# Grouped-query projection of seven token tiles in three rounded products

## The chip, the cores and the metric

The kernel runs on one core of one Trainium2 chip. The metric is the device time of one execution in microseconds (us); the median of three timed executions is what counts. The core has four computing engines that run their own instruction streams side by side and meet at semaphores: TensorE (PE in the rows; PEld is its loading of the stationary operand), VectorE (DVE), ScalarE (ACT) and GpSimd (POOL). SyncE (SP) issues the DMA transfers. Each engine works strictly in the order in which its instructions are written: one that waits holds all behind it.

## What is computed

The reference is one step of a two-layer network on 1024 sample tokens and 128 prompt tokens, all in float32. Each layer normalises its input, projects it with one wide matrix and hands slices of the result to four mixers: latent attention, grouped-query attention, differential attention and a long convolution. Cut to the part that matters here:

```python
h = rmsnorm(x, lp['norm_pre']) * (1.0 + scale) + shift
z = h @ lp['w_in']                         # 1024 input features
(..., g_q, g_k, g_v, g_gate, ...) = jnp.split(z, ...)
gq = rmsnorm(g_q.reshape(b, n, 4, 64), lp['gqa_q_norm'])
gk = rmsnorm(g_k.reshape(b, n, 2, 64), lp['gqa_k_norm'])
gv = g_v.reshape(b, n, 2, 64)
gq, gk = axial_rope(gq, row, col), axial_rope(gk, row, col)   # sample tokens only
o_gqa = gqa_blocks(...)                    # softmax(q k / 8) v
```

The 256 columns of `g_q`, 128 of `g_k` and 128 of `g_v` make one block of 512 output columns. Its product with the normalised tokens is the grouped-query projection.

## The kernel before

**Tiling.** The 1152 tokens are nine tiles of 128 (0 to 7 sample, 8 prompt). The normalised input lies in on-chip memory with features on the partitions, `hT`, eight groups of 128 features by 1152 tokens. Weights come through two slots of 1024 by 512 numbers, `W`. One projection of a tile (`project`, called at line 1247) is eight matmuls of 128x128 against 128x512, one for each feature group, summed in one of eight banks of accumulator memory (`psum`). They are float32 matmuls; a float32 matmul stands in the trace as two records, so a projection is 16 records.

**Stages.** A layer is cut into stages by barriers (`stage_end`) at which the engines wait for each other. The grouped-query stage is from the barrier after the latent attention up to the next one after the grouped-query attention. Tiles 0 and 1 are projected in the last steps of the latent attention stage (line 1043). What follows in the stage on each engine:

- TensorE, lines 1240 to 1261: a gate product of 512 columns (`gate`, 16 records); then for i from 1 to 9 `parts_turned(i - 1)`, eight transposes of the split queries and keys of tile i - 1, and, up to i = 7, `project` of tile i + 1. At i = 9 a second gate product of the same size comes ahead of the transposes. More gate products follow, the transposes of the cached keys, and the attention.
- ScalarE, lines 1667 to 1687: for each tile i, copy the projection out of its bank (384 columns for queries and keys, line 1675, and 128 for values, line 1677), then take the transposed parts of tile i - 1 into `q_parts` and `k_parts` with rounding (lines 1653 to 1661).
- VectorE, lines 2272 to 2294: for each tile i the chain that makes split queries and keys: squares, sum over heads (2283), the variance (1727), then a wait while GpSimd takes the inverse root, two scalings, the rotation (`rope`, seven instructions), and `split` (2231 to 2256), which ends with the subtraction that lets TensorE's transposes go. A step of `link` waits for the instruction before it. After tile 0 comes the end of a gate (1908).
- GpSimd: clears a part of `k_parts` (2431), then one inverse root for each tile.

All these short helpers record one line: 1722 is any `tensor_tensor` of VectorE, 659 any matmul, 663 any transpose, 2336 any `tensor_tensor` of GpSimd, 426 the barrier.

**Three rounded products elsewhere.** The output projection at the layer's end (`out_product`, line 1048) does for its token tiles 3 to 8 what the change does for the grouped-query projection. A float32 number is taken as the sum of a rounded part (type float32r, made by a ScalarE copy) and a rest (made by a VectorE subtraction, also float32r), and the product is high x high + high x low + low x high, three float32r matmuls in place of one float32 matmul, each a single record. `w_high` and `w_low` are the parts of the weights, `o_high` and `o_low` those of the tokens; lines 1500 and 1509 round, lines 2093 and 2102 subtract.

Of the kernel before, what the change touches and what calls it, by code (L numbers as in the profile page):

```python
# [31 lines left out]
F32 = mybir.dt.float32  # L32
# [5 lines left out]
P = 128  # L38
# [11 lines left out]
WC = 512  # L50
# [77 lines left out]
ROPE_DIFF = (DQ + 128, SPLIT + 2 * 896)  # L128
CKEY_DIFF = SPLIT + 2 * 896 + NT * 128
# [218 lines left out]
def program(nc, I, outs, known=None):  # L348
    with ExitStack() as ctx:  # L349
# [28 lines left out]
        o_low = pieces_of("o_low", [(SGH + TT * GW + slot * D, P) for slot in range(3)], KD)  # L378

# [272 lines left out]
        def _(pe):  # L652
# [33 lines left out]
            for l in S.layers():  # L686
# [131 lines left out]

                def gate(grp, c, c0, f, i, banks):

                    weights(c)
                    tok, n = PARTS[i]
                    ps = claim(("gate", grp, f, i), banks)
                    for k in range(KD):
                        last = mm(ps[:, 0:n], W[:, SLOT[c, 0], k, c0 + f * P:c0 + (f + 1) * P],
                                  hT[:, k, tok:tok + n], k == 0, k == KD - 1)
                    last.then_inc(*K.done(("gate", grp, f, i)))
# [409 lines left out]
                for grp in ("gqa", "diff0", "diff1"):  # L1237
                    vg = "gqa_gate" if grp == "gqa" else "diff_vg"
                    vg0, f = (0, 0) if grp == "gqa" else (GW, int(grp[4]))
                    gate(grp[:4], vg, vg0, f, 0, K.next())  # L1240
                    for i in range(1, TT + 1):
                        if i == TT:
                            gate(grp[:4], vg, vg0, f, 1, K.next())
                        parts_turned(grp, i - 1)
                        t = i + AHEAD[grp] - 1
                        if t < TT and grp == "gqa":
                            project(grp, "proj", t, grp, 0, 512, K.next())
                        elif t < TT:
                            diff_project(grp, t, K.next())
                        elif t == TT and grp == "diff0":  # L1250
                            prompt_values()
# [36 lines left out]
        def _(act):  # L1288
# [14 lines left out]
            for l in S.layers():  # L1303
# [136 lines left out]
                def attention(grp):  # L1440
# [32 lines left out]
                    for g in range(tail_step(grp)):  # L1473
# [5 lines left out]
                        if late(grp, g):  # L1479
                            take(g - 2, 0)  # L1480

# [164 lines left out]
                for grp in ("gqa", "diff0", "diff1"):  # L1646
# [19 lines left out]
                    order = six if grp == "gqa" else [(int(grp[4]), i) for i in range(3)]  # L1666
                    for i in range(TT + 1):
                        if i < TT:
# [46 lines left out]
        def _(v):  # L1715
# [39 lines left out]
            for l in S.layers():  # L1755
# [501 lines left out]

                for grp, nh, n in (("gqa", 6, 64), ("diff0", 8, 32), ("diff1", 8, 32)):
# [6 lines left out]
                    if grp == "diff0":  # L2265
# [5 lines left out]
                        link(nc.vector.tensor_scalar(gcol[:, :], gcol[:, :], lamv[:, 5:6], 0.5, ALU.mult, ALU.mult))  # L2271
                    for i in range(TT + 1):
                        if i == TT:
# [262 lines left out]
```

## Time and profile before

| | us |
|---|---|
| median of three timed runs (2438.95 to 2441.79) | 2441.25 |
| profiled execution | 2435.95 |
| its span, first to last instruction | 2434.2 |
| grouped-query stage of layer 0, start to the second gate product | 598.5 to 662.8 |
| the same of layer 1 | 1800.0 to 1864.3 |

A profile lists what each engine did and when, in us from the start of the span. "Busy" is the time in which an instruction of that engine ran; matmuls are pipelined, so their records overlap, and the pace of a row of matmuls is read from their starts. In a timeline a row is: start, length, engine, line, operation, what is written and read with its size, the count of merged instructions, and in brackets how long the engine had been idle and what released it.

### The profile page before, as it was taken

The page shows a single profiled execution, that of the slowest core. Times are in us where ns is not written, and L with a number is a line of the kernel's source. Part 1 is how long each engine was busy: PE and PEld are TensorE (multiplying, and loading weights), DVE is VectorE, ACT ScalarE, POOL GpSimd, SP SyncE. Part 2 cuts the span into 40 slices and gives each one's busy share as a digit, 9 for nine tenths or more (in the row PEclk, how much of TensorE's full clock was granted, in tenths as well). Part 3 has the DMA queues.
Part 4 walks back from the last instruction along what each step waited for, and adds up shares of the span by engine and source line. Part 5 has one row for each costly group of instructions (what it writes and reads, how often), then busy time and mean ns, then how long its engine had stood idle before and what let it go on. Part 6 is the DMA issues. An engine that isn't in the chain of part 4 may idle for free. (4 is left out here: it accounts for less than half of the span.)

```text
span 2434.2 us, 36385 instructions
## 1 busy us (share of the span) xinstructions
PE 2272.0 (93%) x14536; PEld 1599.2 (66%) x14536; DVE 1317.5 (54%) x2454; ACT 935.4 (38%) x1924; POOL 253.8 (10%) x400
## 2 busy tenths in 40 slices
PE   6999999899999998989999999998999999889898
PEld 3656865685477776864856577657854777768657
DVE  3642764564656466583446337545645654855732
ACT  2332113553155265483224221135521652744721
POOL 0310001000100011011304000010011000110213
PEclk9999999999999999999989999999999999999999
DMA  8710100100020000113275101001001100001022
GB/s 282 262 46 29 57 18 1 54 2 15 2 76 2 4 4 7 36 36 131 79 233 203 53 11 57 18 1 54 1 15 37 41 1 8 1 7 71 1 87 87
DMA packets 75150, 129.64 MB, mean 53 GB/s; under 512 B 25794, under 2 KB 38978, under 8 KB 73348
## 3 DMA queue, kind: packets, MB, share of 16 engines
q1 hardware_dynamic: 73960, 121.65, 14.6%
q10 hardware_dynamic: 1024, 5.67, 0.7%
q8 instruction: 117, 1.92, 0.3%
q14 instruction: 49, 0.40, 0.1%
HBM read 110.10 MB, written 21.92 MB: 54 GB/s over the span
## 5 line engine op out<-in xcount | busy, mean ns | idle before, releaser
L659 PE MATMUL psum<-arena 128*32 128x128 f32 (+9 forms) x9392 | 1505.3, 391 | 63.0 <-issue 11.9
L659 PEld LDWEIGHTS psum<-arena 128*32 128x32 f32 (+3 forms) x9392 | 930.5, 151 | 564.5 <-issue 423.7
L663 PE MATMUL psum<-ident,arena 128*128 128x128 f32 (+1 forms) x2248 | 335.2, 279 | 70.8 <-ACT arena L1543 34.0
L1722 DVE TENSOR_TENSOR arena<-arena 128x256 f32<-128x256 f32 (+10 forms) x710 | 318.8, 493 | 146.6 <-ACT arena L1419 42.6
L663 PEld LDWEIGHTS psum<-ident,arena 128*128 128x128 f32 (+1 forms) x2248 | 254.3, 141 | 155.6 <-issue 101.9
L659 PE MATMUL psum<-k_parts,q_parts 96*128 96x384 f32 (+2 forms) x1000 | 269.8, 366 | 17.1 <-ACT arena L1454 6.0
L2019 DVE TENSOR_REDUCE st<-psum 128x1 f32<-128x1152 f32 (+1 forms) x144 | 177.9, 1237 | 52.3 <-PE psum L659 52.1
L1722 DVE TENSOR_TENSOR arena<-psum,arena 128x512 f32<-128x512 f32 (+2 forms) x116 | 68.1, 596 | 253.3 <-PE psum L659 253.1
L2114 DVE TENSOR_REDUCE st<-psum 128x1 f32<-128x1152 f32 (+1 forms) x144 | 174.0, 1235 | 53.6 <-PE psum L659 53.1
L659 PEld LDWEIGHTS psum<-k_parts,q_parts 96*128 96x128 f32 (+1 forms) x1000 | 171.0, 193 | 34.7 <-issue 16.8
L1454 ACT ACTIVATE arena<-psum,st 128x1152 f32<-128x1152 f32 (+1 forms) x144 | 162.4, 1128 | 51.8 <-DVE st L2019 43.7
L1529 ACT ACTIVATE arena<-psum,st 128x1152 f32<-128x1152 f32 (+1 forms) x144 | 162.5, 1129 | 34.0 <-DVE st L2114 33.6
L1469 ACT COPY arena<-psum 128x512 f32<-128x512 f32 (+1 forms) x244 | 102.1, 433 | 184.9 <-PE psum L663 184.8
L2336 POOL TENSOR_TENSOR st<-st,minus 128x1 f32<-128x1 f32 x72 | 43.7, 607 | 798.2 <-ACT arena L1529 798.2
L2336 POOL TENSOR_TENSOR arena<-arena 128x1024 f32<-128x1024 f32 (+2 forms) x38 | 98.6, 2603 | 189.1 <-DVE arena L1855 138.7
L2033 DVE COPY arena<-psum 128x512 f32<-128x512 f32 (+1 forms) x156 | 93.6, 612 | 28.7 <-PE psum L663 28.7
L1543 ACT COPY arena<-psum 128x512 f32<-128x512 f32 (+1 forms) x200 | 90.3, 470 | 46.4 <-PE psum L663 45.4
L1886 DVE SCALAR_TENSOR_TENSOR arena<-arena,hcw 128x1024 f32<-128x1024 f32 x24 | 30.8, 1285 | 125.9 <-ACT arena L1373 125.5
L2124 DVE SCALAR_TENSOR_TENSOR arena<-arena,st 128x1152 f32<-128x1152 f32 (+1 forms) x72 | 93.0, 1291 | 9.8 <-POOL st L2336 9.8
L1492 ACT ACTIVATE arena<-psum 128x512 f32<-128x512 f32 x36 | 21.5, 598 | 173.3 <-PE psum L659 173.3
L2336 POOL TENSOR_TENSOR st<-st,mhalf 128x1 f32<-128x1 f32 (+2 forms) x72 | 56.2, 780 | 300.8 <-DVE st L1727 300.8
L1653 ACT CAST q_parts<-psum 96x512 fp32r<-96x512 f32 (+1 forms) x54 | 31.7, 588 | 117.0 <-PE psum L663 116.5
(146 smaller groups left out, 1685.8 us busy)
## 6 DMA issues: line engine op xcount, KB each, us to landing
arena<-in_ada_w SPq DMA_DIRECT2D x12, 2048.0 KB, 8.3
arena<-in_w_in SPq DMA_DIRECT2D x10, 2048.0 KB, 9.6
arena<-out_xs SPq DMA_DIRECT2D x36, 512.0 KB, 5.9
out_xs<-arena SPq DMA_DIRECT2D x18, 512.0 KB, 2.6
arena<-in_w_out SPq DMA_DIRECT2D x4, 2048.0 KB, 8.0
out_xs<-in_x ACTq DMA_DIRECT2D x1, 4608.0 KB, 19.2
spectrum_kept<-arena SPq DMA_DIRECT2D x2, 2304.0 KB, 8.6
arena<-spectrum_kept SPq DMA_DIRECT2D x2, 2304.0 KB, 8.4
```

The source lines that it names most:

```text
L659: return nc.tensor.matmul(out, lhsT, rhs, start=start, stop=stop)
L663: return nc.tensor.transpose(out, src, ident[0:n, 0:n])
L1454: nc.scalar.activation(at(buf, nk, w), psum[:, 512 * b0:512 * (b0 + nk)].rearrange("p (c n) -> p c n", c=nk)[:, :, 0:w], ACT.Exp, bias=st[ ...
L1469: nc.scalar.copy(at(SLOTS[grp] + slot(grp, u) * 1152 + 512 * j, nk * P), bank[b][:, 0:nk * P]).then_inc(*S.up("turned_scalar", (grp, number)))
L1529: nc.scalar.activation(at(buf, nk, w), psum[:, 512 * b0:512 * (b0 + nk)].rearrange("p (c n) -> p c n", c=nk)[:, :, 0:w], ACT.Exp, bias=st[ ...
L1543: nc.scalar.copy(at(SLOTS[grp] + slot(grp, u) * 1152 + 512 * j, nk * P), bank[b][:, 0:nk * P]).then_inc(*S.up("turned_scalar", (grp, number)))
L1722: return nc.vector.tensor_tensor(out, a, b, op)
L2019: nc.vector.tensor_reduce(st[:, 16 + x % 4:17 + x % 4], psum[:, 512 * b0:512 * (b0 + nk)].rearrange("p (c n) -> p c n", c=nk)[:, :, 0:w], ...
L2033: nc.vector.tensor_copy(at(SLOTS[grp] + slot(grp, u) * 1152 + 512 * j, nk * P), bank[b][:, 0:nk * P]).then_inc(*S.up("turned_vector", (grp ...
L2114: nc.vector.tensor_reduce(st[:, 16 + x % 4:17 + x % 4], psum[:, 512 * b0:512 * (b0 + nk)].rearrange("p (c n) -> p c n", c=nk)[:, :, 0:w], ...
L2124: nc.vector.scalar_tensor_tensor(p0, p1, c, p0, ALU.mult, ALU.add).then_inc(*S.up("mixed", (grp, u)))
L2336: return nc.gpsimd.tensor_tensor(out, a, b, op)
```

## The change

The projections of the grouped-query block for tiles 2 to 8 (seven of nine) are made as three rounded products. Tiles 0 and 1 stay as they were.

- ScalarE rounds the weight block in two parts of 128x2048 in the last steps of the latent attention, and each token tile (128x1024) in the grouped-query stage: tile 2 ahead of the loop, tile i + 3 at the head of step i, behind a wait for the product of tile i + 1, whose buffer it takes.
- VectorE subtracts: at the stage's start the rest of tile 2 (two instructions of 128x512) and of the weights (two of 128x2048), which overwrite the weights in `W`, and at the head of step i, for i from 1 to 6, the rest of tile i + 2 (two of 128x512).
- TensorE makes 24 float32r matmuls for a tile. The product of tile 2 now stands right behind the first gate product, ahead of the transposes of tile 0, and the product of tile i + 2 (before: i + 1) behind the transposes of tile i - 1.

```diff
@@ tensor engine @@
+                def gqa_project(t, banks):
+                    for part in range(2):
+                        pe.wait_ge(*S.at("gqa_w_low", part))
+                    pe.wait_ge(*S.at("gqa_h_low", t))
+                    ps = claim(("proj", "gqa", t), banks)
+                    for k in range(KD):
+                        wh, wl = (w[k // 4][:, k % 4, :] for w in (gqa_w_high, gqa_w_low))
+                        hh, hl = gqa_h_high[t % 2][:, k, :], gqa_h_low[t % 2][k // 4][:, k % 4, :]
+                        mm(ps[:, :], hh, wh, k == 0, False)
+                        mm(ps[:, :], hh, wl, False, False)
+                        last = mm(ps[:, :], hl, wh, False, k == KD - 1)
+                    last.then_inc(*K.done(("proj", "gqa", t)))
...
                     gate(grp[:4], vg, vg0, f, 0, K.next())
+                    if grp == "gqa":
+                        gqa_project(GQA_SPLIT, K.next())
                     for i in range(1, TT + 1):
...
                         parts_turned(grp, i - 1)
-                        t = i + AHEAD[grp] - 1
+                        t = i + GQA_SPLIT if grp == "gqa" else i + AHEAD[grp] - 1
                         if t < TT and grp == "gqa":
-                            project(grp, "proj", t, grp, 0, 512, K.next())
+                            gqa_project(t, K.next())
@@ scalar engine @@
+                        if grp == "mla" and len(units) + 1 <= g < len(units) + 3:
+                            gqa_round_weights(g - len(units) - 1)
+                def gqa_round_tokens(t):
+                    if t >= GQA_SPLIT + 2:
+                        act.wait_ge(*K.full(("proj", "gqa", t - 2)))
+                    nc.scalar.copy(gqa_h_high[t % 2][:, :, :], hT[:, :, t * P:(t + 1) * P]).then_inc(*S.up("gqa_h_high", t))
...
+                    if grp == "gqa":
+                        gqa_round_tokens(GQA_SPLIT)
                     for i in range(TT + 1):
+                        if grp == "gqa" and i + GQA_SPLIT + 1 < TT:
+                            gqa_round_tokens(i + GQA_SPLIT + 1)
@@ vector engine @@
+                def gqa_weights_rest(part):
+                    v.wait_ge(*S.at("gqa_w_high", part))
+                    v.wait_ge(*K.full(("proj", "gqa", GQA_SPLIT - 1)))
+                    tt(gqa_w_low[part][:, :, :], W[:, SLOT["gqa", 0], 4 * part:4 * part + 4, :],
+                       gqa_w_high[part][:, :, :].bitcast(F32), ALU.subtract).then_inc(*S.up("gqa_w_low", part))
+                def gqa_tokens_rest(t):
+                    v.wait_ge(*S.at("gqa_h_high", t))
+                    for part in range(2):
+                        ks = slice(4 * part, 4 * part + 4)
+                        last = tt(gqa_h_low[t % 2][part][:, :, :], hT[:, ks, t * P:(t + 1) * P],
+                                  gqa_h_high[t % 2][:, ks, :].bitcast(F32), ALU.subtract)
+                    last.then_inc(*S.up("gqa_h_low", t))
...
+                    if grp == "gqa":
+                        gqa_tokens_rest(GQA_SPLIT)
+                        for part in range(2):
+                            gqa_weights_rest(part)
                     for i in range(TT + 1):
+                        if grp == "gqa" and 1 <= i < TT - GQA_SPLIT:
+                            gqa_tokens_rest(i + GQA_SPLIT)
```

VectorE's stream at the start of the grouped-query stage, before (line 1722 is a `tensor_tensor`, the rows run from the end of the latent attention into the chain of tile 0):

```order
L1722 TENSOR_TENSOR arena<-psum,arena 128x128
L2053 SCALAR_TENSOR_TENSOR arena<-arena,psum 128x128
L1722 TENSOR_TENSOR arena<-arena 128x384
L2283 TENSOR_REDUCE st<-arena 128x6
L1727 TENSOR_SCALAR st<-st 128x6
```

The same place after the change, with line 1766 in the part of 1722 and 2097 in that of 2053; `gqa_h_high` and `gqa_h_low` are the parts of a token tile, `gqa_w_high` and `gqa_w_low` those of the weights:

```order
L1766 TENSOR_TENSOR arena<-psum,arena 128x128
L2097 SCALAR_TENSOR_TENSOR arena<-arena,psum 128x128
L1766 TENSOR_TENSOR gqa_h_low_0_75<-arena,gqa_h_high_73 128x512
L1766 TENSOR_TENSOR gqa_h_low_1_76<-arena,gqa_h_high_73 128x512
L1766 TENSOR_TENSOR gqa_w_low_71<-arena,gqa_w_high_69 128x2048
L1766 TENSOR_TENSOR gqa_w_low_72<-arena,gqa_w_high_70 128x2048
L1766 TENSOR_TENSOR arena<-arena 128x384
L2349 TENSOR_REDUCE st<-arena 128x6
L1771 TENSOR_SCALAR st<-st 128x6
```

Four instructions now stand ahead of the chain of tile 0.

VectorE's stream where tile 0 ends and tile 1 begins, after the change (before, the first four of these rows are followed at once by the `128x384` row):

```order
L2297 CAST split_buf<-arena 128x2x64
L2299 SCALAR_TENSOR_TENSOR split_buf<-arena,split_buf 128x4x64
L1766 TENSOR_TENSOR split_buf<-arena,split_buf 128x2x64
L1952 SCALAR_TENSOR_TENSOR arena<-arena,psum 128x512
L1766 TENSOR_TENSOR gqa_h_low_0_77<-arena,gqa_h_high_74 128x512
L1766 TENSOR_TENSOR gqa_h_low_1_78<-arena,gqa_h_high_74 128x512
L1766 TENSOR_TENSOR arena<-arena 128x384
```

The rest of tile 3 stands between the split of tile 0 and the chain of tile 1, and so on for each tile up to 6.

TensorE's stream at the start of the stage, before (16 matmuls are the product of tile 1 and the gate product, with the barrier between them; the matmuls out of `split_buf` are the transposes of tile 0; the last row is the product of tile 2):

```order
L659 MATMUL psum<-arena 128x512 x16
L663 MATMUL psum<-ident,split_buf 128x128 x5
L663 MATMUL psum<-ident,split_buf 64x128
L663 MATMUL psum<-ident,split_buf 128x128
L663 MATMUL psum<-ident,split_buf 64x128
L659 MATMUL psum<-arena 128x512 x8
```

And after the change (line 668 in the part of 659, 672 in that of 663; the three kinds of rows repeat for the eight feature groups where "..." stands):

```order
L668 MATMUL psum<-arena 128x512 x16
L668 MATMUL psum<-gqa_w_high_69,gqa_h_high_73 128x512
L668 MATMUL psum<-gqa_w_low_71,gqa_h_high_73 128x512
L668 MATMUL psum<-gqa_w_high_69,gqa_h_low_0_75 128x512
...
L668 MATMUL psum<-gqa_w_high_70,gqa_h_low_1_76 128x512
L672 MATMUL psum<-ident,split_buf 128x128 x5
L672 MATMUL psum<-ident,split_buf 64x128
L672 MATMUL psum<-ident,split_buf 128x128
L672 MATMUL psum<-ident,split_buf 64x128
```

The product of tile 2 has moved from behind the transposes of tile 0 to ahead of them, and is 24 matmuls.

## Rows read from the trace of the kernel before

**Rows 1.** The page's busy times, share of the span, instructions:
```profile
PE 2272.0 (93%) x14536; PEld 1599.2 (66%) x14536; DVE 1317.5 (54%) x2454; ACT 935.4 (38%) x1924; POOL 253.8 (10%) x400
```

**Rows 2.** Busy time by stretch: us; PE, PEld, DVE, ACT, POOL; granted clock; DMA share, GB/s:
```profile
598.50:662.80 64.30, 62.90 (x193) 30.49 (x194) 43.86 (x130) 15.11 (x42) 12.90 (x10) 1.00 0.01 2
1800.00:1864.30 64.30, 62.86 (x192) 30.44 (x193) 43.86 (x129) 15.09 (x42) 12.90 (x10) 1.00 0.01 2
```

**Rows 3.** Timeline of TensorE, layer 0, from the stage's start to its transposes:
```profile
598.66 7.11 PE L659 MATMUL psum<-arena 128*128 128x512 f32 x16 [0.26 <-PEq L426]
...
606.74 1.09 PE L663 MATMUL psum<-ident,split_buf 128*128 128x128 f32 x8 [0.97 <-DVE split_buf L1722]
607.67 7.03 PE L659 MATMUL psum<-arena 128*128 128x512 f32 x16
...
655.04 7.03 PE L659 MATMUL psum<-arena 128*128 128x512 f32 x16
661.91 1.04 PE L663 MATMUL psum<-ident,split_buf 128*128 128x128 f32 x8
662.79 7.03 PE L659 MATMUL psum<-arena 128*128 128x512 f32 x16
```

**Rows 4.** Timeline of VectorE, one tile of the same stretch:
```profile
647.00 0.56 DVE L1722 TENSOR_TENSOR arena<-arena 128x384 f32<-128x384 f32 x1 [0.99 <-ACT arena L1677]
...
649.79 0.56 DVE L1722 TENSOR_TENSOR arena<-arena,st 128x384 f32<-128x384 f32 x1 [1.44 <-POOL st L2336]
...
653.78 0.28 DVE L1722 TENSOR_TENSOR split_buf<-arena,split_buf 128x128 fp32r<-128x128 f32 x1
```

**Rows 5.** Timeline of TensorE, output projection, rounded products of layer 0:
```profile
1153.15 0.40 PE L659 MATMUL psum<-w_high,o_high 128*128 128x512 f32 x1
...
1168.14 0.39 PE L659 MATMUL psum<-w_high,o_high 128*128 128x512 f32 x1
```

**Rows 6.** Roundings and rests, by tile: count, min/median/max ns, first and last start:
```profile
L1500 ACT CAST w_high<-arena x8: 1882/1892/1911, 1123.8 to 2353.8; 128x2048 fp32r<-128x2048 f32 x8
L1509 ACT CAST o_high<-arena x12: 1037/1042/1047, 1141.3 to 2404.2; 128x1024 fp32r<-128x1024 f32 x12
L1722 DVE TENSOR_TENSOR w_low<-arena,w_high x8: 2278/2289/3179, 1145.9 to 2362.4; 128x2048 fp32r<-128x2048 f32 x8
L1722 DVE TENSOR_TENSOR o_low<-arena,o_high x12: 1211/1216/1221, 1143.4 to 2406.7; 128x1024 fp32r<-128x1024 f32 x12
```

**Rows 7.** Lines by form: busy us, mean ns of one, idle before:
```profile
L1722 DVE TENSOR_TENSOR arena<-arena 128x512 f32<-128x512 f32 x52 | 34.0, 685 | 27.6 <-ACT arena L1553 27.6
```

**Rows 8.** Timeline of ScalarE around the barrier, and a later tile:
```profile
590.13 0.27 ACT L1469 COPY arena<-psum 128x128 f32<-128x128 f32 x1 [6.71 <-PE psum L663]
598.48 0.48 ACT L1675 COPY arena<-psum 128x384 f32<-128x384 f32 x1 [8.08 <-PEq L426]
598.86 0.27 ACT L1677 COPY arena<-psum 128x128 f32<-128x128 f32 x1
...
662.12 0.48 ACT L1675 COPY arena<-psum 128x384 f32<-128x384 f32 x1 [6.19 <-PE psum L659]
```

**Rows 9.** Timeline of VectorE at the stage's start and behind tile 0:
```profile
599.26 0.56 DVE L1722 TENSOR_TENSOR arena<-arena 128x384 f32<-128x384 f32 x1 [7.26 <-ACT arena L1677]
...
606.40 0.28 DVE L1722 TENSOR_TENSOR split_buf<-arena,split_buf 128x128 fp32r<-128x128 f32 x1
606.60 0.68 DVE L1908 SCALAR_TENSOR_TENSOR arena<-arena,psum 128x512 f32<-128x512 f32 x1
607.20 0.55 DVE L1722 TENSOR_TENSOR arena<-arena 128x384 f32<-128x384 f32 x1
```

**Rows 10.** Timeline of GpSimd at the stage's start, and beside a weight rest:
```profile
598.51 2.38 POOL L2431 MEMSET k_parts<- 64x1280 f32 x2 [147.07 <-PEq L426]
...
1143.63 3.21 POOL L2336 TENSOR_TENSOR arena<-arena 128x1024 f32<-128x1024 f32 x1 [1.58 <-DVE arena L2084]
```

**Rows 11.** Busy time by stretch, grouped-query attention of layer 0:
```profile
690.00:760.00 70.00, 67.57 (x674) 53.96 (x676) 47.70 (x60) 43.66 (x82) 0.00 (x0) 1.00 0.11 34
```

More of the change, by code:

```diff
@@ L128 @@
 ROPE_DIFF = (DQ + 128, SPLIT + 2 * 896)
+GQA_SPLIT = 2
+GQA_W_HIGH = KB
+GQA_H_HIGH = (KB + 4096, TH["gqa"] + 1024)
+GQA_H_LOW = ((SPLIT + 2 * 896, SPLIT + 2 * 896 + 512), (TH["gqa"] + 2048, OT + 4 * TOK + 1792))
 CKEY_DIFF = SPLIT + 2 * 896 + NT * 128
@@ L378, in program @@
         o_low = pieces_of("o_low", [(SGH + TT * GW + slot * D, P) for slot in range(3)], KD)
+        gqa_w_high = pieces_of("gqa_w_high", [(GQA_W_HIGH + part * 2048, WC) for part in range(2)], 4)
+        gqa_w_low = pieces_of("gqa_w_low", [(W0 + part * 2048, WC) for part in range(2)], 4)
+        gqa_h_high = pieces_of("gqa_h_high", [(off, P) for off in GQA_H_HIGH], KD)
+        gqa_h_low = [pieces_of(f"gqa_h_low{slot}_", [(off, P) for off in offs], 4) for slot, offs in enumerate(GQA_H_LOW)]
         def at(off, *shape, parts=P, base=0):
@@ L1480, in attention, with gqa_round_weights @@
                             take(g - 2, 0)
+                        if grp == "mla" and len(units) + 1 <= g < len(units) + 3:
+                            gqa_round_weights(g - len(units) - 1)
+                def gqa_round_weights(part):
+                    act.wait_ge(*S.at(f"weights{SLOT['gqa', 0]}_loaded", ("gqa", 0)))
+                    act.wait_ge(*S.at("scores", ("mla", len(UNITS["mla"]) - 1)))
+                    nc.scalar.copy(gqa_w_high[part][:, :, :], W[:, SLOT["gqa", 0], 4 * part:4 * part + 4, :]
+                                   ).then_inc(*S.up("gqa_w_high", part))
+                def gqa_round_tokens(t):
+                    if t >= GQA_SPLIT + 2:
+                        act.wait_ge(*K.full(("proj", "gqa", t - 2)))
+                    nc.scalar.copy(gqa_h_high[t % 2][:, :, :], hT[:, :, t * P:(t + 1) * P]).then_inc(*S.up("gqa_h_high", t))
                 def out_square(t, half):
```

## The prediction

> **What bounds the kernel now.** The page says TensorE is busy for 93% of the span and VectorE for 54% [rows 1], which suggests that any saving on TensorE is a saving in time. That is an average, so I read the stretch that is changed: from the barrier that opens the grouped-query stage to the second gate product. In its 64.3 us TensorE is busy for 62.9 and VectorE for 43.9 [rows 2]. The timeline of TensorE shows a steady pace: from the product of tile 2 (start 607.67) to the second gate product (662.79) seven products and seven sets of transposes take 55.12 us, 7.87 us a tile, without an idle mark [rows 3]. TensorE sets the pace, but I ask how near the next engine is. The timeline of VectorE answers it: the chain of one tile runs from 647.00 to the start of its last instruction at 653.78, 6.78 us, of which 1.44 is a wait for GpSimd's inverse root in the middle. Ahead of it VectorE had waited 0.99 us until ScalarE had copied the projection out [rows 4]. The 43.9 us busy hide this: the waits inside the chain cannot be used, since the engine works in order. VectorE's own period is 6.78 plus 0.21 to the next start (606.40 to 606.60 [rows 9]) = 6.99 us. The slack for a tile is 7.87 - 6.99 = 0.88 us. That number decides the case.
>
> **What TensorE saves.** A float32 product starts at 655.04 and its transposes at 661.91 [rows 3]: 6.87 us for 16 records. In the output projection the rounded matmul of the same size comes every (1168.14 - 1153.15) / 66 = 0.227 us [rows 5] (66 matmuls lie between the two rows); 24 of them are 5.45 us. So each product is 1.42 us shorter, seven products 9.9 us, both layers 19.9 us. It is a saving in time only if nothing else becomes later.
>
> **What VectorE gets.** In each step a rest of 128x1024 in two halves. A `tensor_tensor` of 128x512 from on-chip memory takes 0.685 us [rows 7], but its successor starts earlier than it ends: the gate end of 0.68 us at 606.60 is followed at 607.20 [rows 9], a step of 0.60. Two are 1.20 us. The one-piece rest of the same size took 1.216 us [rows 6], so 1.20 is neither low nor high; the bounds are 1.13 (1.216 less the same overlap) and 1.37 (twice 0.685). At the stage's start come four more instructions: rest of tile 2, 1.20, and the weights, two at 2.289 [rows 6], which with the same overlap advance the stream by 2 x 2.20 = 4.40. One such rest beside GpSimd took 3.18 [rows 6, 10]; this is the upper bound for one of them.
>
> **The new pace.** With the rest, VectorE needs 6.99 + 1.20 = 8.19 us for a tile, TensorE 7.87 - 1.42 = 6.45. The slower one rules: 8.19, which is 0.32 more than the 7.87 of before. The saved matmul time turns into a wait of TensorE for `split_buf`: on its engine the next product is queued behind the waiting transposes, and then the gate product.
>
> **The sum, along VectorE's line in layer 0.** ScalarE's first instruction behind the barrier starts at 598.48 [rows 8]; it is now the rounding of tile 2, 1.04 us [rows 6], and VectorE reacts 0.13 later, as it did to the copy that ended at 599.13 (599.26 [rows 8, 9]): 599.65. Then
>
> - rest of tile 2 and of the weights: 1.20 + 4.40, to 605.25 (before, tile 0 began here at 599.26);
> - tile 0 and the gate end behind it: 6.99 + 0.60, to 612.84;
> - six times rest and tile, tiles 1 to 6: 6 x 8.19 = 49.14, to 661.98;
> - tile 7 has no rest; its last instruction starts 6.78 later, at 668.76;
> - the transposes start 0.34 behind that (606.40 to 606.74 [rows 3, 9]) and the gate product 0.88 behind them (661.91 to 662.79 [rows 3]): 669.98.
>
> Before it started at 662.79, so layer 0 loses 7.2 us. From there on TensorE has four long gate products in a row, and the chain of tile 8, done by about 675, is hidden behind the first; nothing is late and nothing is won. In layer 1 the same stretch has the same length and the same busy times to 0.05 us [rows 2], so it loses the same. Together 14.4 us.
>
> **What is hidden.** The two roundings of the weights (2 x 1.89 us [rows 6]) stand in ScalarE's stream behind its last copy at 590.13, and the barrier lets it go on at 598.48 [rows 8]: 3.8 us in 8.1 of idle time, cost nothing; without that cover they would cost their length. The waits on weights and scores that they add are on events that had happened. The product of tile 2 can start once the first gate product is done (598.66 + 6.87 = 605.5) and the weights' rest is there (605.25 + 0.09): no wait worth a number. The seven roundings of tokens take 7.3 us of ScalarE's idle time, but stand ahead of the copy that VectorE waits for; that is the second rival. DMA carries nothing of this.
>
> **A rule on the shared port.** GpSimd's clearing of `k_parts` runs from 598.51 to 600.89 [rows 10], beside the first rest. A `tensor_tensor` with both inputs in on-chip memory ran beside it at 599.26 in its usual 0.56 us [rows 4, 9]; I take no cost. But one weight rest that began beside the addition of GpSimd (1143.63 to 1146.84 [rows 10]) took 3.18 in place of 2.29 [rows 6]. If the clearing held up the first rest in the same way, VectorE would start it at 600.89 in place of 599.65, and both layers would take 2.5 us more: 16.9. The Trainium skill (GPSIMD Engine Reference, 1. Specifications) says that GpSimd's access to on-chip memory is shared with VectorE and that instructions with two inputs there contend with it. By that rule it is 16.9, by the row 14.4; the second decides since it is the same operation beside the same clearing.
>
> **The rivals.**
> 1. The saving goes through (faster). TensorE stays the bound, -19.9 us: 2421. It wants VectorE's tile with its rest under 6.45 us; the chain alone is 6.99. Even a free rest would leave 7.87 - 6.99 = 0.88 a tile. Chance 0.03.
> 2. ScalarE closes a ring. The copy of projection i + 1 now stands behind the rounding of tile i + 4, which waits for the product of tile i + 2, which waits for its rest, and that follows the split of tile i - 1. From one split to the one two tiles on: rest and reaction 1.57, product 5.45, ScalarE's reaction 0.22 (655.04 + 6.86 to 662.12 [rows 3, 8]), rounding 0.95, copies to VectorE's start 0.68, chain 6.78: 15.65 us for two tiles, against VectorE's 16.38. It decides from 0.73 us more. If it is 2 us longer than I count, each tile takes 0.64 more, 12 tiles 7.6 us: 2463. Chance 0.08.
> 3. The rests are cheap (no change). If they ran at half my durations, a layer would lose 7.2 - (7 x 0.6 + 2.2) = 0.8 us and the kernel end at 2443. The rests of the output projection speak against it [rows 6]. Chance 0.08.
> 4. TensorE's clock. The granted clock was 1.00 of the 2.4 GHz level in this stage [rows 2]; now TensorE idles 1.5 to 1.9 us of every 8.2. In the grouped-query attention it waits often and shortly, and the clock stays 1.00 [rows 11]. If products ran at the lower level, the ring of rival 2 would be 5.45 longer, 21.1 us for two tiles, 2.4 a tile over mine: up to 28 us, 2484. The Trainium skill (TensorE: Matmul & The Clock Gate, A second HAM failure mode) says that frequent small idles between groups of matmuls can make the clock swing; the attention's row speaks against it. Chance 0.05.
>
> **How the numbers follow.** The profiled execution took 2435.95 us, 0.2% under the median of 2441.25; I add the difference to both: 2450.4 for a profiled one and 2441.25 + 14.4 = 2455.7 for the median. The forecast has a chance of 0.76 and its own range is 2449 to 2461: the rest between 1.13 and 1.37 is -1.0 to +2.4 us (14 pairs), the port +2.5, the pace of two or three timed runs another 2. The range for 8 in 10 goes to 2447 and 2464. What a measurement of this kernel can tell from no change is about 0.2%, 4.9 us. Faster by more: 0.03 (rival 1). Within: 0.08 (rival 3). Slower: 0.76 + 0.08 + 0.05 = 0.89.
>
> **What would show it.** In the profile after, TensorE waits before the transposes of each of tiles 1 to 7 for VectorE's line in `split_buf`, some 1.5 us each, and before most products some 0.3 us for the rest. VectorE shows no wait for ScalarE at a tile's head; if it does, rival 2 is at work. The second gate product starts near 670.0 (669 to 673) with the products at 5.45 us and the clock at 1.00. The prediction is wrong if VectorE's step is under 7.9 us, or if something behind the gate product gives the time back.

## The result: the kernel got slower, by about what the forecast said

The changed kernel takes 2457.47 us (median of five, 2454.76 to 2468.1) against 2441.25 before; the ratio is 1.0085 with a 95% interval of 1.0057 to 1.0114. The forecast was 2455.7, slower, range 2447 to 2464. The profiled execution took 2454.76 us, its span is 2452.9 against 2434.2: +18.7, where the sum said +14.4.

The page's busy times after the change (those of before: [rows 1]) and the stretch from the stage's barrier to the attention's start, layer 0, in the columns of [rows 2]:

```profile
PE 2264.1 (92%) x14648; PEld 1624.9 (66%) x14648; DVE 1340.5 (55%) x2486; ACT 955.3 (39%) x1942; POOL 253.7 (10%) x400
```
```profile
602.00:702.00 100.00, 83.05 (x340) 55.76 (x340) 62.53 (x164) 27.16 (x62) 14.20 (x11) 0.97 0.07 24
```

TensorE is busy for 8 us less in all, and is idle for 17 of the stage's 100 us. Where it waits, its timeline shows (products left out; compare [rows 3]):

```profile
602.14 7.11 PE L668 MATMUL psum<-arena 128*128 128x512 f32 x16 [0.26 <-PEq L435]
...
615.93 1.09 PE L672 MATMUL psum<-ident,split_buf 128*128 128x128 f32 x8 [1.20 <-DVE split_buf L1766]
...
665.53 1.09 PE L672 MATMUL psum<-ident,split_buf 128*128 128x128 f32 x8 [1.07 <-DVE split_buf L1766]
672.49 1.97 PE L672 MATMUL psum<-ident,split_buf 128*128 128x128 f32 x8 [5.87 <-DVE split_buf L1766]
674.25 8.28 PE L668 MATMUL psum<-arena 128*128 128x512 f32 x16
682.36 1.04 PE L672 MATMUL psum<-ident,split_buf 128*128 128x128 f32 x8
```

Each of the first seven sets of transposes waits 1.0 to 1.2 us for VectorE (forecast some 1.5), and that of tile 7, ahead of which no product stands any more, 5.87 us. Behind this wait the transposes take 1.97 us and not 1.09, and the gate product 8.28 and not 7.03. VectorE's timeline of the head of the stage and of one step:

```profile
603.14 1.29 DVE L1766 TENSOR_TENSOR gqa_h_low<-arena,gqa_h_high 128x512 fp32r<-128x512 f32 x2 [7.66 <-ACT gqa_h_high L1520]
604.35 4.49 DVE L1766 TENSOR_TENSOR gqa_w_low<-arena,gqa_w_high 128x2048 fp32r<-128x2048 f32 x2
608.75 0.55 DVE L1766 TENSOR_TENSOR arena<-arena 128x384 f32<-128x384 f32 x1
...
649.05 1.28 DVE L1766 TENSOR_TENSOR gqa_h_low<-arena,gqa_h_high 128x512 fp32r<-128x512 f32 x2
650.26 0.55 DVE L1766 TENSOR_TENSOR arena<-arena 128x384 f32<-128x384 f32 x1
...
657.22 1.28 DVE L1766 TENSOR_TENSOR gqa_h_low<-arena,gqa_h_high 128x512 fp32r<-128x512 f32 x2
```

A step is 657.22 - 649.05 = 8.17 us (forecast 8.19), the two rests advance the line by 1.21 (1.20), and no row at a tile's head waits for ScalarE (in [rows 4] it waited 0.99): in the loop of layer 0 VectorE's only wait is the 1.4 us for GpSimd inside each chain. In layer 1 it waits for ScalarE too, twice, each time behind a product that ran while the granted clock was down (6.9 and 6.8 us from its first matmul to the start of its last, in place of 5.3). The two rows of VectorE and TensorE's clock in that stretch:

```profile
1839.22 0.56 DVE L1766 TENSOR_TENSOR arena<-arena 128x384 f32<-128x384 f32 x1 [1.05 <-ACT arena L1721]
...
1856.60 0.56 DVE L1766 TENSOR_TENSOR arena<-arena 128x384 f32<-128x384 f32 x1 [0.95 <-ACT arena L1721]
```
```profile
1820.00:1830.00 10.00, 8.14 (x36) 5.70 (x34) 8.26 (x21) 3.24 (x7) 1.32 (x1) 1.00 0.00 0
1830.00:1840.00 10.00, 9.74 (x39) 7.84 (x40) 7.24 (x21) 2.47 (x7) 1.32 (x1) 0.83 0.00 0
```

**How to measure.** I use the stretch from TensorE's first matmul behind the barrier to the attention's first matmul, "the stage" below. Everything that was changed lies in it. The total holds more: in stages that no kernel here changes, the granted clock differs from execution to execution. In the latent attention of layer 0, ahead of the change, it was 0.95 before and 0.73 after, and the changed kernel's profiled execution, 0.3 us late at 448 us, is 3.5 us late behind it:

```profile
445.00:470.00 25.00, 19.70 (x112) 16.27 (x112) 12.62 (x17) 14.72 (x27) 0.29 (x1) 0.95 0.28 99
```
```profile
445.00:470.00 25.00, 20.93 (x85) 17.09 (x85) 9.96 (x13) 11.76 (x21) 0.29 (x1) 0.73 0.30 105
```

And the stretch from the last group's attention in layer 1 to the output projection's first rounded product took 291.2 us before, at a granted clock of 0.96, and 283.9 after, at 1.00, with the same instructions. Single totals are therefore good to some 7 us at best; the changed kernel's own five differ by 13. The stage figures come from one profiled execution of each kernel. They agree to some tenths between the layers where the clock behaves alike in both, and differ by up to 2.5 us where it does not (changed kernel, without weight rests).

| kernel | stage, layer 0 / 1 | timed median | ratio to before (95%) |
|---|---|---|---|
| before | 91.1 / 91.0 | 2441.25 | |
| changed | 100.2 / 102.7 | 2457.5 | 1.0085 (1.0057 to 1.0114) |
| float products | 103.0 / 102.6 | 2457.0 | 1.0062 (1.0045 to 1.0080) |
| no token rests | 96.8 / 96.8 | 2445.7 | 1.0028 (1.0019 to 1.0037) |
| no weight rests | 99.6 / 102.1 | 2455.6 | 1.0065 (1.0050 to 1.0080) |
| gate ahead | 98.4 / 98.3 | 2461.4 | 1.0089 (1.0074 to 1.0104) |
| fill the wait | 100.3 / 100.3 | 2452.0 | 1.0051 (1.0038 to 1.0064) |
| GpSimd's rests | 106.9 / 106.9 | 2473.9 | 1.0135 (1.0108 to 1.0162) |
| spread gates | 82.7 / 82.7 | 2416.8 | 0.9901 (0.9888 to 0.9913) |
| spread, copy first | 82.7 / 82.7 | 2416.9 | 0.9901 (0.9886 to 0.9915) |
| before, spread | 90.1 / 90.1 | 2436.6 | 0.9981 (0.9971 to 0.9991) |

The ratios are to runs of the kernel before on the same chip (medians 2438.3, 2440.0 and 2441.7 in the three groups).

### The profile page after: what moved, and what is told of

Its sections match the earlier page's. It is cut to its first block and busy times, and to the rows that moved or that the text cites. A ratio compares the mean times of both kernels' runs of the same rounds, so it can differ in the third digit from the quotient of the medians.

```text
span 2452.9 us, 36693 instructions
## 1 busy us (share of the span) xinstructions
PE 2264.1 (92%) x14648; PEld 1624.9 (66%) x14648; DVE 1340.5 (55%) x2486; ACT 955.3 (39%) x1942; POOL 253.7 (10%) x400
## 5 line engine op out<-in xcount | busy, mean ns | idle before, releaser
L668 PE MATMUL psum<-arena 128*32 128x256 f32 (+9 forms) x9168 | 1407.2, 385 | 62.8 <-ACT arena L1327 11.9
L668 PEld LDWEIGHTS psum<-arena 128*32 128x32 f32 (+3 forms) x9168 | 889.0, 149 | 517.8 <-issue 377.7
L672 PE MATMUL psum<-ident,arena 128*128 128x128 f32 (+1 forms) x2248 | 333.8, 278 | 71.3 <-ACT arena L1583 34.6
L668 PEld LDWEIGHTS psum<-k_parts,q_parts 96*128 96x128 f32 (+1 forms) x1000 | 169.4, 192 | 33.9 <-issue 16.7
L2402 POOL TENSOR_TENSOR arena<-arena 128x1024 f32<-128x1024 f32 (+2 forms) x38 | 98.4, 2598 | 187.3 <-DVE arena L1899 137.2
```

Of the source, the lines that this page charges most:

```text
L668: return nc.tensor.matmul(out, lhsT, rhs, start=start, stop=stop)
L672: return nc.tensor.transpose(out, src, ident[0:n, 0:n])
L2402: return nc.gpsimd.tensor_tensor(out, a, b, op)
```

## The experiments

**Are the shorter products worth anything?** All roundings and rests stay, only the product is eight float32 matmuls again.

```diff
-                        mm(ps[:, :], hh, wh, k == 0, False)
-                        mm(ps[:, :], hh, wl, False, False)
-                        last = mm(ps[:, :], hl, wh, False, k == KD - 1)
+                        last = mm(ps[:, :], hT[:, k, t * P:(t + 1) * P], wh.bitcast(F32), k == 0, k == KD - 1)
```

> The changed kernel with all its roundings and rests, but the seven products are made by eight plain float32 matmuls again (tokens unrounded, against the rounded part of the weights; the two other products are left out, so the result is less exact). Stretch measured: first matmul behind the barrier that opens the grouped-query stage to the transposes of tile 8; before 71.0 us in both layers, changed kernel 80.2 and 82.7. Theory (VectorE's line of one chain and one rest a tile sets the pace, 8.17 us): a product longer by 1.42 us is nearly hidden, only the ring over ScalarE (17.1 us for two tiles against 16.4) may take 0.3 us a tile; stretch 80 to 82.5 us, total within 4 us of the changed kernel. Rival (the shorter products do save time and something else costs it): stretch longer by 7 x 1.42 = 10 us, 90 to 92, total +20 us.

Up to the transposes of tile 8 it is 83.0 and 82.6 us, up to half a microsecond over my range, and the total is that of the changed kernel. Products longer by 10 us a layer cost 2.8 us in layer 0: 2.1 up to the transposes of tile 7, and 0.7 in the gate product behind them, which ran longer at the low clock. In layer 1 they cost nothing, but that comparison flatters them, since only the changed kernel had the low clock inside its loop there. So the theory holds and the rival falls: at least 7 of the 9.9 us that the shorter products save turn into waiting time in the changed kernel. The ring over ScalarE is seen at work; in VectorE's timeline two of the tiles wait for the copy:

```profile
627.66 0.56 DVE L1764 TENSOR_TENSOR arena<-arena 128x384 f32<-128x384 f32 x1 [0.67 <-ACT arena L1719]
...
644.93 0.56 DVE L1764 TENSOR_TENSOR arena<-arena 128x384 f32<-128x384 f32 x1 [0.66 <-ACT arena L1719]
```

**Is it VectorE's rests of the tokens?** They are left out, the matmuls stay as many, and the product waits for the rounded tokens in place of their rest.

```diff
-                    pe.wait_ge(*S.at("gqa_h_low", t))
+                    pe.wait_ge(*S.at("gqa_h_high", t))
...
-                        last = mm(ps[:, :], hl, wh, False, k == KD - 1)
+                        last = mm(ps[:, :], hh, wh, False, k == KD - 1)
...
-                        gqa_tokens_rest(GQA_SPLIT)
...
-                        if grp == "gqa" and 1 <= i < TT - GQA_SPLIT:
-                            gqa_tokens_rest(i + GQA_SPLIT)
```

> The changed kernel without the rests of the token tiles on VectorE (14 instructions of 128x512 a layer); the third product takes the rounded tokens again in place of their rest, so the result is not exact, the matmuls are as many. Theory with VectorE's line alone: the step falls from 8.17 to 6.99 us, the stretch by 8.4 us a layer, total -17 us. Theory with the ring over ScalarE (product, rounding, copy, chain: 15.3 us for two tiles without the rest) as the next bound: step 7.66 us, the stretch 4.4 us shorter, total about -9 us, and VectorE waits 0.7 us a tile for ScalarE. If VectorE is not the bound: no change.

The stage is 3.4 and 5.9 us shorter, 9.3 in all, and the median 11.7 us lower. The five steps from the transposes of tile 1 to those of tile 6 take 39.3 us, 7.85 each, far from VectorE's 6.99. One product among them ran while the granted clock was down (6.95 us from first to last matmul in place of 5.3). The pairs of steps behind it, at a clock of 1.00, take 15.34 us, 7.67 each: the ring's 7.66. The waits for the copy are now large:

```profile
612.08 0.56 DVE L1766 TENSOR_TENSOR arena<-arena 128x384 f32<-128x384 f32 x1 [2.26 <-ACT arena L1721]
...
629.04 0.56 DVE L1766 TENSOR_TENSOR arena<-arena 128x384 f32<-128x384 f32 x1 [2.94 <-ACT arena L1721]
```

VectorE is the bound, and right behind it comes the ring. Even with the token rests left out the stage stays 5.8 us longer than before; the weights' rests, the order and the clock behind the wait of 5.87 us are still in it.

**And the rests of the weights?** They are left out, likewise.

```diff
-                        pe.wait_ge(*S.at("gqa_w_low", part))
+                        pe.wait_ge(*S.at("gqa_w_high", part))
...
-                        mm(ps[:, :], hh, wl, False, False)
+                        mm(ps[:, :], hh, wh, False, False)
...
-                        for part in range(2):
-                            gqa_weights_rest(part)
```

> The changed kernel without the rests of the weights on VectorE (two instructions of 128x2048 a layer at the stage's start); the second product takes the rounded weights again, so the result is not exact, the matmuls are as many. Theory (VectorE's line is the path from the stage's start on): each layer 4.4 us shorter, total -9 us, step unchanged at 8.17. Rival (the first gate product of 6.9 us covers the weights' rests): no change, since product 2 starts at 6.9 us in either case.

A miss: 0.6 us a layer, not 4.4. VectorE starts tile 0 earlier and then waits at tile 1:

```profile
616.54 0.56 DVE L1766 TENSOR_TENSOR arena<-arena 128x384 f32<-128x384 f32 x1 [2.93 <-ACT arena L1721]
```

That copy stands behind the rounding of tile 4, which waits for the product of tile 2, which now stands ahead of everything: first gate product and product of tile 2 together 12.41, ScalarE's reaction 0.20, rounding 0.95, copy to VectorE's start 0.67, which is 616.54 - 602.31 = 14.23 us. In the changed kernel VectorE gets to tile 1 at 617.59 - 602.14 = 15.45, before it did at 607.20 - 598.66 = 8.54. So of the 6.9 us that the stage's start loses, the weights' rests alone are answerable for 1.2 (and in layer 0 half of that goes again in the gate product behind the long wait, 8.7 us here for 8.1). A further 3.2 (4.4 less 1.2) stand on two paths, the weights' rests and the order on TensorE and ScalarE, and would go only if both were changed. The last 2.5 are by estimate VectorE's own: the rests of tiles 2 and 3, 1.2 each, and the wait for the first rounding, 0.4, less 0.3. No run changes the order without the spreading below, so this division of the 5.7 is worked out and not shown. I had charged 4.4 us to one path where a second was 1.2 us behind it. From tile 1 to the last split of tile 7 the changed kernel needs 54.6 us and the one before 54.3. The loop gained and lost next to nothing, 0.3 us; in layer 0 the whole loss is at its start and at its end.

**The wait ahead of tile 7.** One move: the second gate product goes ahead of the transposes of tile 7.

```diff
-                        if i == TT:
+                        if i == (TT - 1 if grp == "gqa" else TT):
                             gate(grp[:4], vg, vg0, f, 1, K.next())
```

> The changed kernel with one move on TensorE: the second gate product stands ahead of the transposes of tile 7 in place of those of tile 8, and fills the wait of 5.87 us that stands there. Everything is computed. Theory (the hole ahead of tile 7 costs its own product's time, and the granted clock falls behind it, so that transposes and gate take 2 us more): the transposes of tile 8 then start when VectorE's chain of tile 8 is done, 75.5 us from the stage's start in place of 80.2 and 82.7; total -9 to -12 us, the clock 1.00 behind it. Rival (the clock alone): the hole moves and costs the same, total within 3 us.

The place is hit, 75.5 us in both layers, but only 1.8 and 4.4 us of it reach the attention, and nothing shows in the total: its ratio to before is that of the changed kernel (1.0089 and 1.0085), where I expected 9 to 12 us less. TensorE's timeline says why the stage gained so little:

```profile
674.32 1.04 PE L672 MATMUL psum<-ident,split_buf 128*128 128x128 f32 x8
678.60 1.97 PE L672 MATMUL psum<-ident,split_buf 128*128 128x128 f32 x8 [3.24 <-DVE split_buf L1766]
680.36 19.53 PE L668 MATMUL psum<-arena 128*128 128x128 f32 x64
```
```profile
680.00:690.00 10.00, 10.00 (x33) 6.55 (x32) 0.98 (x2) 1.74 (x5) 0.00 (x0) 0.77 0.64 216
```

The wait moved to tile 8 and shrank to 3.24 us, and the granted clock fell behind it all the same, now over the gate products: 19.53 us where they take 17.47 at the full clock. My expectation of a clock of 1.00 there was wrong; the rival was half right.

**Is it the wait that lowers the clock?** TensorE gets more to do: in the wait ahead of tile 7 it makes six matmuls of the gate product for nothing and later the product in full.

```diff
+                        if grp == "gqa" and i == TT - 2:
+                            ps_gate = claim(("gate", "gqa", 0, 1), K.next())
+                            for k in range(6):
+                                mm(ps_gate[:, :], W[:, SLOT[vg, 0], k, 0:P], hT[:, k, 512:1024], k == 0, k == 5)
```

> The changed kernel with more work on TensorE: in its wait ahead of the transposes of tile 7 it makes six of the eight matmuls of the second gate product, 5.2 us, and throws them away; the product is made in full at its place as before. Everything is computed. Theory (the wait itself costs nothing more than VectorE's delay, but the granted clock falls to the lower level behind it, for the transposes and the gate product): the transposes take 1.04 us and the gate product 7.0 in place of 1.97 and 8.3 to 8.6; the stage is 2 to 3.5 us a layer shorter, total -4 to -7 us against the changed kernel though more is computed. Rival (the clock falls for another reason, or the waits of 1 to 2 us a tile are enough): no change.

```profile
665.15 5.32 PE L668 MATMUL psum<-arena 128*128 128x512 f32 x12
671.18 1.09 PE L672 MATMUL psum<-ident,split_buf 128*128 128x128 f32 x8 [0.71 <-DVE split_buf L1775]
672.11 7.03 PE L668 MATMUL psum<-arena 128*128 128x512 f32 x16
```

With 0.71 us of wait in place of 5.87 the transposes take 1.09 and the gate 7.03 us, in both layers: the drop of the clock comes from the long wait. So it is in all ten stages recorded here that have a wait of 5.75 to 5.87 us at this place: the transposes behind it take 1.97 us and the gate product 7.6 to 9.2. From the transposes of tile 7 to the attention it is 27.8 us, against 29.9 and 30.2 in the changed kernel: 2.1 and 2.4 us a layer. The median is 5.5 us lower (ratio 1.0051 against 1.0085). The stage of layer 0 is no shorter, though, where 2 to 3.5 us were expected, since here both layers had the low clock inside the loop that the changed kernel had in layer 1 only (transposes of tile 7 at 72.5 us, not 70.3). What decides whether a layer gets that dip I haven't settled: it stands in one of two layers of the changed kernel and of the one without weight rests, in both here and in both of the one without token rests, in neither of the one with the gate ahead.

**Can GpSimd take the rests?** Its inverse root keeps it busy 1.3 us a tile.

```diff
-                        if grp == "gqa" and 1 <= i < TT - GQA_SPLIT:
-                            gqa_tokens_rest(i + GQA_SPLIT)
...
                     inverse_root(("heads", t), st[:, 8 * (t % 2):8 * (t % 2) + 6])
+                    u = t + GQA_SPLIT + 1
+                    if u < TT:
+                        pool.wait_ge(*S.at("gqa_h_high", u))
+                        for part in range(2):
+                            ks = slice(4 * part, 4 * part + 4)
+                            last = tt(gqa_h_low[u % 2][part][:, :, :], hT[:, ks, u * P:(u + 1) * P],
+                                      gqa_h_high[u % 2][:, ks, :].bitcast(F32), ALU.subtract)
+                        last.then_inc(*S.up("gqa_h_low_pool", u))
```

> The changed kernel with the rests of tiles 3 to 8 made by GpSimd behind its inverse root in place of VectorE. Everything is computed. GpSimd is free for some 6 us a tile; an addition of 128x1024 took it 2.4 us alone. Theory without contention: VectorE's step falls to that of the kernel without token rests (7.7 us on average), stage 96 to 98 us, total some 6 to 10 us under the changed kernel. Rival (the two engines keep each other from on-chip memory): VectorE's two-input instructions stand still while GpSimd works, step 9 us or more, stage 106 us or more, total slower than the changed kernel by 8 us or more.

The contention decides, 106.9 us. Both engines' timeline of one tile:

```profile
631.88 2.85 POOL L2400 TENSOR_TENSOR gqa_h_low<-arena,gqa_h_high 128x512 fp32r<-128x512 f32 x2
631.95 1.64 DVE L1766 TENSOR_TENSOR arena<-arena,st 128x384 f32<-128x384 f32 x1 [1.44 <-POOL st L2400]
633.62 3.39 DVE L1766 TENSOR_TENSOR arena<-arena 128x384 f32<-128x384 f32 x7
```

Beside 2.85 us of GpSimd, VectorE's instructions take 1.64 in place of 0.56 and 3.39 in place of 2.42: 2.05 us more, where the rest it was spared costs 1.21. Over six tiles that makes 5.0 us of the 6.4 by which the transposes of tile 7 come later than in layer 0 of the changed kernel; the other 1.2 are two waits for ScalarE's copy, behind products at the low clock.

This run also has a row that limits what a wait says of the clock:

```profile
1891.83 1.09 PE L672 MATMUL psum<-ident,split_buf 128*128 128x128 f32 x8 [3.42 <-DVE split_buf L1766]
```

The granted clock stayed at 1.00 over the next 10 us, and in layer 0 behind a wait of 3.43 us at the same place too. In the kernel with the gate ahead a wait of 3.24 us was followed by the low clock in both layers, and here one of 3.27 ahead of the transposes of tile 0 was too (0.83 from 619 to 629 us). Between 3.2 and 3.5 us the length of the wait does not decide by itself, and no run shows what does.

**Filling the waits.** If VectorE's line is the bound and TensorE waits, TensorE's other work of the stage belongs into the waits. The gate products are cut into pieces of 128 tokens and laid in; three gates' ends on ScalarE and VectorE move into the loops; gates take banks 6 and 7, the rest 0 to 5.

```diff
+                        for piece in range(4):
+                            gate_piece(0, 0, piece)
+                        gqa_project(GQA_SPLIT, K.front())
+                        gate_piece(*next(spread))
+                        for i in range(1, TT + 1):
+                            parts_turned(grp, i - 1)
+                            if i + GQA_SPLIT < TT:
+                                gqa_project(i + GQA_SPLIT, K.front())
+                            for _ in range((1, 1, 1, 1, 1, 1, 3, 2, 2)[i - 1]):
+                                gate_piece(*next(spread))
...
+                        if grp == "gqa" and i in (4, 5, 8):
+                            gate_tanh("gqa", *order[{4: 1, 5: 2, 8: 3}[i]], order)
...
+                        if grp == "gqa" and i in (4, 5, 8):
+                            gate_finish("gqa", *order[{4: 1, 5: 2, 8: 3}[i]], order, og)
```

> The changed kernel with the gate products of the grouped-query stage cut into pieces of 128 tokens (1.7 us each) and laid into TensorE's waits: one piece behind each product, three behind the transposes of tile 6, two behind those of tile 7 and of tile 8; ScalarE's and VectorE's part of three gates moves into their loops. Everything is computed. From the barrier to the attention's first matmul it was 91.0 us before, 100.2 and 102.7 in the changed kernel. Theory (VectorE's line sets the pace, TensorE waits 1.8 us a tile plus 5.9 us ahead of tile 7, and the clock falls behind that wait): the pieces cost nothing in the waits, VectorE's line gets 0.85 us longer, no wait over 2 us is left and the clock stays 1.00; 82 to 84 us, 7 to 9 less than before; total 2422 to 2428, faster than both kernels. Rival (the stage's length is given by something else, as ScalarE's ring): no gain over the changed kernel but the hole's, 96 us or more, total 2445 or more.

82.7 us in both layers, 8.3 less than before, and 2416.8 in all, 1% faster than the kernel before and below the range expected; the stages account for 16.7 us of the 23.2 between the medians on the same chip, the profiled span is 17.8 lower, and what is left is no more than executions of one kernel differ by (before, on that chip: 2438.65 to 2445.03). TensorE's timeline has no wait above 0.44 us left up to the last transposes, and the clock stays up:

```profile
666.05 1.95 PE L668 MATMUL psum<-arena 128*128 128x128 f32 x16
667.83 1.04 PE L672 MATMUL psum<-ident,split_buf 128*128 128x128 f32 x8
668.70 5.52 PE L668 MATMUL psum<-arena 128*128 128x128 f32 x48
674.24 1.09 PE L672 MATMUL psum<-ident,split_buf 128*128 128x128 f32 x8
675.17 3.74 PE L668 MATMUL psum<-arena 128*128 128x128 f32 x32
679.35 1.09 PE L672 MATMUL psum<-ident,split_buf 128*128 128x128 f32 x8 [0.44 <-DVE split_buf L1794]
```
```profile
603.00:686.00 83.00, 80.42 (x533) 72.28 (x534) 62.26 (x164) 27.49 (x62) 14.16 (x11) 1.00 0.07 23
```

TensorE is busy for 80.4 of 83 us, and VectorE is still at 8.17 us a tile, 8.4 to 8.8 where the end of a gate stands between two tiles. Both bounds now nearly meet.

**Does the ring still bind there?** One move more on ScalarE.

> As e5_spread, and ScalarE copies each projection out ahead of rounding the next tile, not behind it. Theory of the ring over ScalarE (VectorE waited for the copy in the trace of the changed kernel where the clock was low, and in the kernel without token rests): the ring is 1.0 us shorter for two tiles. If VectorE's line alone is the bound: within 1 us of e5_spread in the stage; if the ring binds in e5_spread: up to 0.5 us a tile, 3 us a layer shorter.

```diff
-                        if grp == "gqa" and i + GQA_SPLIT + 1 < TT:
-                            gqa_round_tokens(i + GQA_SPLIT + 1)
...
                             ins.then_inc(*K.drained(job))
+                        if grp == "gqa" and i + GQA_SPLIT + 1 < TT:
+                            gqa_round_tokens(i + GQA_SPLIT + 1)
```

Within 0.1 us in every set of transposes: with the clock up the ring is not the bound.

**Is it the spreading alone?** The same spreading in the kernel before, with its float32 products.

> The kernel before, with its float32 products, and only the spreading of e5_spread: gate products in pieces of 128 tokens between the products and transposes, and the gates' ends in the loops. Everything is computed. Theory (TensorE is the bound there and has no waits to fill; what e5_spread won is the shorter products): barrier to attention 90 to 92 us as before (91.0), each of the first tiles 9.6 us apart in place of 7.9 and the rest earlier, total within 3 us of the kernel before. Rival (the spreading alone makes e5_spread fast): 83 to 85 us, total 2424 to 2428.

90.1 us in the stage, 0.9 less than before, 2436.6 in all, 5.1 under the kernel before on the same chip where I expected at most 3. The first tiles are 9.53 us apart, as they must be with a piece of gate in each, and TensorE is as full as it was. Of the 8.3 us that the spread version wins in a stage, 0.9 belong to the order and 7.4 to the shorter products, of a possible 9.9.

## Why the prediction was right, point by point

- **VectorE's step, 8.19 us, as the new pace.** Measured 8.17; the slack of 0.88 us in [rows 4, 9] against a rest of 1.20 was the deciding comparison. Confirmed by the kernels without token rests and with float products. What the comparison decided is that the saving of 9.9 us a layer came to nothing; the loss itself is made at the stage's start and end, since the loop took 54.6 us for 54.3.
- **TensorE's saving, 5.45 for 6.87 us.** The products are that short (24 matmuls 0.227 us apart) and of the 9.9 us a layer at most 2.8 were worth anything in time: confirmed by the float products.
- **The sum along VectorE's line.** VectorE began tile 0 at 608.75 - 602.14 = 6.6 us from the barrier (forecast 605.25 - 598.66 = 6.6), and the gate product started at 72.1 us against 71.3 forecast. The number was right, in part by luck; the reading that the start's 5.6 us of rests alone cause the delay was not: a second path, product 2 and ScalarE's rounding, is only 1.2 us shorter, as the kernel without weight rests shows. It stood in my ring (rival 2), but I had applied that to the loop only.
- **Nothing late behind the gate product, and the clock at 1.00.** This step failed. The wait ahead of tile 7 (5.87 us) follows from the sum, but I did not list it, since I looked at the waits of 1.5 us a tile. Behind it the granted clock is at its low level for part of the time (0.80 over 672.5 to 683.0): transposes 0.8 and gate 1.2 us longer in layer 0, 0.9 and 1.6 in layer 1. With the two waits of layer 1 (2.0 us) the stage loses 9.1 and 11.7 where 7.2 and 7.2 were forecast. 14.4 + 2.0 + 2.5 + 2.0 = 20.9 us, against 20.8 measured. The rest of the kernel gave 2.1 back by its clock in this execution, so that the span came out 18.7 us longer, and the median 16.2. That the total lies 1.8 us from the forecast is luck: the stages lost 6.4 us more than the sum has.
- **Rivals.** The saving going through (1) and cheap rests (3) are out. The ring (2) exists, with 7.67 us a tile at the full clock for 7.66 worked out without a rest, and binds where the clock is low or the rest is gone. The clock (4) was real, but small: 28 us were its ceiling, and some 4.5 of direct cost and 2 by the ring were seen.
- **The shared port.** The first rest ran beside GpSimd's clearing (601.99 to 604.37) in its usual 1.29 us for two, and the weights' rests in 4.49: the cost of zero was right for a clearing, and the 2.5 us more that the rival reading gave did not come. For a subtraction of GpSimd beside it the Trainium skill's rule (GPSIMD Engine Reference, 1. Specifications) holds, with 2.05 us lost for 2.85. On the clock, the Trainium skill (TensorE: Matmul & The Clock Gate, A second HAM failure mode) spoke of small idles between groups; the dip of layer 1 at 0.83 with waits of 1 to 2 us fits it, and the attention's row [rows 11], on which I relied, did not speak for this stage.

## What to carry to other kernels

Before the bound engine is relieved, the period of the next engine is to be read, with its waits inside a chain counted in; here it was 0.88 us a tile away and the relief itself cost it 1.2. A saving on an engine that now waits is not lost but unused: moving its other work into the waits in pieces of their size turned a kernel 0.85% slower than before into one 1% faster. And a wait of nearly 6 us cost twice each time, once for itself and once by the clock behind it.

## What was not expected of the hardware

A single wait of 3.24 us on TensorE was followed by a low granted clock, 0.77 from 680 to 690 us (gate products 19.5 in place of 17.5 us), yet one of 3.42 us in another kernel was not. One of 5.87 was followed by transposes and a gate product together 1.4 to 3 us longer; with useless matmuls in the wait the clock stayed. GpSimd's work can cost VectorE more than it takes off it: 2.85 us of GpSimd's two-input subtraction lengthened VectorE's chain by 2.05 and spared it 1.21, while its clearing of 2.38 us cost nothing that could be seen.
